# Hybrid decoder step: compression and block scores with their operands turned, one projection split in two roundings, constants in two loads

## The reference

```python
h = rms(x, norm1) * (1 + sc1) + sh1          # sc1, sh1 from c @ w_ada
z = h @ w_in                                  # 2856 columns: gq gk gv ga gr nq kc vc ks vs kw vw ng
log_a = log_sigmoid(ga @ w_gla_a + b_gla_a) / 16
o_g, state = gla(gq * 64 ** -0.5, gk, gv, log_a, state_gla)   # 4 heads, chunks of 16 tokens
o_g = rms(o_g, gla_norm) * silu(gr)
kc_c = rms(compress(kc, w_ck), kc_norm)       # blocks of 32 rows, step 16: 31 for the prompt
vc_c = compress(vc, w_cv)                     # einsum('bnjgd,jde->bnge', blocks, w)
o_n = g0 * cmp(qn, kc_c, vc_c) + g1 * selected(qn, ks, vs) + g2 * window(qn, kw, vw)   # g = sigmoid(ng)
x = x + g1_ * (concat(o_g, rms(o_n, nsa_norm)) @ w_out)
h2 = rms(x, norm2) * (1 + sc2) + sh2
x = x + g2_ * ((gelu(conv(h2 @ w_up)) * (h2 @ w_gate)) @ w_down)
```

## Time and profile before

| | us |
|---|---|
| three runs, lowest, median, highest | 997.56, 1007.92, 1012.57 |
| profiled execution, its own time | 995.57 |
| its span in the trace | 993.5 |
| PE busy in the span | 922.9 (93%) |
| DVE, ACT, POOL busy | 350.6, 356.7, 312.5 |
| mean granted PE clock | 0.955 |

### The profile page before, as it was taken

The page is one execution under the profiler, slowest core; times in us unless marked ns, Lnnn a source line. Parts: engine busy times, 40 slices in busy tenths (PEclk is TensorE's granted clock), DMA queues, the critical chain, the costliest instruction groups (busy, mean ns, idle before and its releaser), DMA issues.

```text
span 993.5 us, 16849 instructions
## 1 busy us (share of the span) xinstructions
PE 922.9 (93%) x6771; PEld 761.6 (77%) x6771; DVE 350.6 (35%) x816; ACT 356.7 (36%) x739; POOL 312.5 (31%) x235
## 2 busy tenths in 40 slices
PE   2899999999987999897879999999999999899998
PEld 0444667677875454665659989999999999899997
DVE  2207214423656788534242163222222222300001
ACT  4123134421332677547152354333333333212120
POOL 0003030402509100070633644334343331524240
PEclk9999989997875799999989999999999999999999
DMA  9922622304093700285826403222233332253430
GB/s 318 346 129 85 207 89 86 131 11 160 2 290 60 234 1 1 79 260 161 223 81 213 127 23 105 86 85 86 85 87 90 95 91 81 60 135 82 128 82 23
DMA packets 129293, 117.27 MB, mean 118 GB/s; under 512 B 13869, under 2 KB 107754, under 8 KB 128986
## 3 DMA queue, kind: packets, MB, share of 16 engines
q1 hardware_dynamic: 124496, 100.64, 33.8%
q0 software_dynamic: 4720, 15.55, 4.8%
HBM read 110.88 MB, written 9.45 MB: 121 GB/s over the span
## 4 chain that ended last, share of the span: by engine, by line
PE 82%; DMA 5%; DVE 5%; ACT 3%; POOL 2%; SPq 2%; issue 1%; DVEq 0%; ACTq 0%; POOLq 0%
PE bank L1507 14%; PE bank L1508 14%; PE bank L1509 14%; PE bank L902 6%; PE bank L1000 6%; PE bank L991 3%; PE bank L1214 3%; PE bank L977 3%; PE bank L984 3%; DMA z<-in_w_ada_dram 2%; PE bank L1314 2%; PE bank L1284 2%; PE bank L1116 1%; PE bank L943 1%; DMA cs<-constants 1%
## 5 line engine op out<-in xcount | busy, mean ns | idle before, releaser
L1508 PE MATMUL bank<-feat_r,ring_r 128*128 128x272 f32 x672 | 193.7, 288 | 0.0
L1507 PE MATMUL bank<-qk_r,ring_r 128*128 128x272 f32 x672 | 193.5, 288 | 0.0
L1509 PE MATMUL bank<-qk_r,ring_r 128*128 128x272 f32 x672 | 193.2, 288 | 0.0
L871 POOL TENSOR_TENSOR ring_r<-ring,ring_r 128x1024 fp32r<-128x1024 f32 x44 | 108.9, 2478 | 146.9 <-ACT ring_r L1943 146.9
L1509 PEld LDWEIGHTS bank<-qk_r,ring_r 128*128 128x128 f32 x672 | 126.5, 188 | 0.0
L1507 PEld LDWEIGHTS bank<-qk_r,ring_r 128*128 128x128 f32 x672 | 126.3, 188 | 0.0
L1508 PEld LDWEIGHTS bank<-feat_r,ring_r 128*128 128x128 f32 x672 | 126.0, 187 | 0.0
L1943 ACT ACTIVATE ring_r<-ring 128x1024 fp32r<-128x1024 f32 x44 | 46.1, 1053 | 88.5 <-DMA ring<-in_w_gate_dram 85.6
L848 POOL DMA_DIRECT2D z<-in_cache_kv_dram x64 | 34.2, 536 | 132.9 <-PE bank L902 93.5
L2557 DVE SCALAR_TENSOR_TENSOR z<-bank,conv,z 128x511 f32<-128x511 f32 x22 | 16.5, 750 | 134.3 <-ACT z L1970 134.3
L902 PE MATMUL bank<-cs,room 128*128 128x128 f32 (+3 forms) x293 | 42.2, 285 | 20.5 <-DMA room<-in_nsa_norm_dram 11.8
...
## 6 DMA issues: line engine op xcount, KB each, us to landing
...
```

The costliest lines, as they stand in the source:

```text
L871: pool.tensor_tensor(rounded(low), low, high_part(high), ALU.subtract).then_inc(u_split, 1)
L1507: pe.matmul(dst, rounded(high), rounded(x_high), start=first, stop=False)
L1508: pe.matmul(dst, rounded(high), rounded(x_low), start=False, stop=False)
L1509: return pe.matmul(dst, rounded(low), rounded(x_high), start=False, stop=last)
```

## The change

Five things change.

- `SPLIT` gets the gqk piece as its first entry. The four gqk units become three products of 8 rounded matmuls, as gv has. ACT rounds the gqk weights before it reads out the first unit, POOL makes their rest, and DVE makes the rest of the features right after unit 3 instead of after unit 8. `sample_rows(0)` and `sample_columns(0)` move from units 8 and 9 to units 0 and 1.
- The gate bias becomes a 17th row of `wga`, with a row of ones as 17th row of `gaT`; L1087 goes.
- The late constants are loaded in two parts. The part behind the states (`STATES` to `CW`, with `pair` in it) is loaded ahead of the ada piece 7; the other part (`dist`, `cbias`, `cmask`, half of `sbias`) stays where the whole was.
- Compression is turned: 32 block columns of `kT` are stationary and 128 columns of `wp` move, the offset j choosing one of four bands. Bands and halves are summed by `fold`; the values need 16 such matmuls. Block scores are turned too: `kcn` is stationary, the queries move in 512 columns into four bands, and the result is copied out and turned back by 8 transposes. `vrep` goes.
- DVE's order around it changes: `praw` and `kcn` come ahead of the norm of the keys, the gates go behind the block scores, and the scaling of the GLA output goes to POOL, behind its last small DMA.

```diff
-                        ("seqmask", NB), ("dist", SEQ), ("cbias", QT * G * R * 32), ("cmask", QT * 32), ("pair", P),
-                        ("sbias", PAST), ("nbias", TURNS * NS), ("wbias", WIN), ("dcbias", NCS + 1),
+                        ("seqmask", NB), ("dist", SEQ), ("cbias", QT * G * R * 32), ("cmask", QT * 32),
+                        ("sbias", PAST), ("pair", P),
...
+STATES = EC + NB * 2 * DV
...
-        gaT = at(5504, TOK, rows=16)
+        gaT = at(5504, TOK, rows=17)
...
-        ROW_NTH = [4, 2, 3, 5, 6, 7]
-        BAND_NTH = 1
-        UH, US, FH = 4 * KD // 2, 4, KD
-        SPLIT = ROWED[2:]
+        ROW_NTH = [1, 3, 4, 5, 6, 7]
+        BAND_NTH = 2
+        UH, US, FH = 5 * KD // 2, 5, KD
+        SPLIT = [ROWED[0]] + ROWED[2:]
...
                 if item == ("a", 7):
                     sp.wait_ge(unit_out, 23)
+                    sp.wait_ge(ld_consts, 16)
+                    sp.dma_start(cs[:, STATES:CW], cst[:, STATES:CW]).then_inc(ld_consts, 16)
                 if item == ("a", 9):
                     sp.wait_ge(*KC2_DONE)
                     load_block_weights()
                 if item == ("a", 10):
                     sp.wait_ge(st_gla, 32)
-                    sp.dma_start(cs[:, EC:CW], cst[:, EC:CW]).then_inc(ld_consts, 16)
+                    sp.wait_ge(ld_consts, 32)
+                    sp.dma_start(cs[:, EC:STATES], cst[:, EC:STATES]).then_inc(ld_consts, 16)
...
+                if n == 6:
+                    ones_row = cst[0:1, CC["tri"][0]:CC["tri"][1]]
+                    sp.dma_start(gaT[16:17, 0:SEQ].rearrange("p (t n) -> p t n", n=P), among(ones_row, QT)).then_inc(ld_small, 16)
+                    sp.dma_start(gaT[16:17, SEQ:TOK], ones_row[:, 0:NS]).then_inc(ld_small, 16)
...
+            pool.wait_ge(mx_act, TILES + 2)
+            for t in range(TILES):
+                m = ROWS[t]
+                og = z[0:m, t, 0:512].rearrange("p (h d) -> p h d", d=DV)
+                pool.tensor_tensor(og, og, spread(gss[0:m, t, 0:H], DV), ALU.mult).then_inc(hb_ok, 1)
...
+                elif dst[0] == "gqk":
+                    i, cols_ = SPLIT.index(n), slice(c0, c0 + width)
+                    for k in range(KD):
+                        pe.wait_ge(fh_ok, k + 1)
+                        pe.wait_ge(u_high_ok, KD // 2 * i + k // 2 + 1)
+                        pe.matmul(b[:, :], rounded(w_in_high(n, k)[:, cols_]), rounded(qk[:, k, 0:SEQ]), start=(k == 0), stop=False)
+                    pe.wait_ge(u_split, i + 1)
+                    for k in range(KD):
+                        pe.matmul(b[:, :], rounded(w_in_raw(n, k)[:, cols_]), rounded(qk[:, k, 0:SEQ]), start=False, stop=False)
+                    for k in range(KD):
+                        pe.wait_ge(fl_ok, k + 1)
+                        last = pe.matmul(b[:, :], rounded(w_in_high(n, k)[:, cols_]), rounded(feat[:, k, 0:SEQ]),
+                                         start=False, stop=(k == KD - 1))
...
                 unit_product(u)
+                if u == 0:
+                    pe.wait_ge(feat_ok, 6)
+                    sample_rows(0)
+                if u == 1:
+                    sample_columns(0)
                 if u == 2:
+                    pe.wait_ge(samp_ok, 1)
...
-                pe.matmul(dst, gaT[:, t * P:t * P + ROWS[t]], wga[:, :], start=True, stop=False)
-                last = pe.matmul(dst, const("tri", 1)[:, 0:ROWS[t]], bga[:, :], start=False, stop=True)
+                last = pe.matmul(dst, gaT[:, t * P:t * P + ROWS[t]], wga[:, :], start=True, stop=True)
...
-                compress(lambda g: bank[b + g][:, 0:32], kv,
-                         lambda part, j: kT[part, kv, j:j + CST * 31 + 1:CST]).then_inc(cmp_pe, 1)
+                for j in range(CST):
+                    for g in range(G):
+                        part, band_ = slice(g * DH, (g + 1) * DH), slice(j % 4 * BAND, (j % 4 + 1) * BAND)
+                        ins = pe.matmul(bank[b + g][band_, 0:P], kT[part, kv, j:j + CST * 31 + 1:CST], wp[kv][part, j, :],
+                                        start=(j < 4), stop=(j >= CST - 4), skip_group_check=True)
+                ins.then_inc(cmp_pe, 1)
...
             compressed(1, 6)
-            pe.wait_ge(cmp_dve, 1)
-            fold(lambda part: bank[6][part, 0:NCP], lambda g, h: praw[:, 1, g, h:h + NCP]).then_inc(cmp_pe, 1)
             pe.wait_ge(ld_wk, 64)
             compressed(0, 4)
+            pe.wait_ge(cmp_dve, 2)
+            for h in range(2):
+                for g in range(G):
+                    last = pe.matmul(bank[4][g * DH:(g + 1) * DH, 0:NCP], praw[:, 0, g, h * DH:(h + 1) * DH],
+                                     const("fold")[:, h:h + NCP], start=(h == 0), stop=(h == 1), skip_group_check=True)
+            last.then_inc(cmp_pe, 1)
+            for g in range(G):
+                for h in range(2):
+                    for r in range(R):
+                        last = pe.matmul(bank[7][r * 32:r * 32 + 32 - h, g * DH:(g + 1) * DH],
+                                         const("fold")[:, h:32], praw[:, 1, g, h * DH:(h + 1) * DH],
+                                         start=(h == 0), stop=(h == 1), skip_group_check=True)
+            last.then_inc(cmp_pe, 1)
+            pe.wait_ge(ld_consts, 32)
+            pe.wait_ge(cmp_dve, 3)
+            pe.matmul(bank[6][:, 0:NCP], const("pair"), ksq[:, 0:NCP], start=True, stop=True).then_inc(cmp_pe, 1)
             pe.wait_ge(kv_ok, 1)
             pe.wait_ge(mod_ok, 9)
             selected_columns(Z_KS, 1)
-            pe.wait_ge(cmp_dve, 3)
-            fold(lambda part: bank[4][part, 0:NCP], lambda g, h: praw[:, 0, g, h:h + NCP]).then_inc(cmp_pe, 1)
-            flip(bank[7][:, 0:P], vrep.rearrange("p a b -> p (a b)")).then_inc(cmp_pe, 1)
             selected_columns(Z_KW, 2)
-            pe.wait_ge(ld_consts, 32)
-            pe.wait_ge(cmp_dve, 4)
-            pe.matmul(bank[6][:, 0:NCP], const("pair"), ksq[:, 0:NCP], start=True, stop=True).then_inc(cmp_pe, 1)
             pe.wait_ge(qT_ok, R + 1)
             for j, c in enumerate((Z_KS, Z_KW)):
                 last = flip(bank[0][:, j * NS:(j + 1) * NS], z[0:NS, QT, c:c + P], NS)
             last.then_inc(k_t, 1)
-            pe.wait_ge(cmp_dve, 6)
-            pe.wait_ge(kT_ok, 5)
-            for t in range(QT):
-                for r in range(R):
-                    for g in range(G):
-                        last = pe.matmul(bank[4 + g][:, t * P + r * 32:t * P + (r + 1) * 32],
-                                         qT[g * DH:(g + 1) * DH, r, t * P:(t + 1) * P],
-                                         kcn[g * DH:(g + 1) * DH, :], start=True, stop=True)
+            pe.wait_ge(cmp_dve, 4)
+            for r in range(R):
+                for g in range(G):
+                    part = slice(g * DH, (g + 1) * DH)
+                    last = pe.matmul(bank[4 + g][r * 32:(r + 1) * 32, :], kcn[part, :], qT[part, r, 0:SEQ],
+                                     start=True, stop=True, skip_group_check=True)
+            last.then_inc(cs_out, 1)
+            pe.wait_ge(cpt_ok, 2)
+            for g in range(G):
+                for t in range(QT):
+                    last = flip(bank[4 + g][:, t * P:(t + 1) * P], cpt[:, g, t * P:(t + 1) * P])
             last.then_inc(cs_out, 1)
 
...
+            weights_high(0)
             for n in range(0, EARLY, 2):
                 unit_out_of_bank(n)
+                if n == 0:
+                    sample_rows_out(0)
...
-            a.wait_ge(cmp_pe, 6)
+            a.wait_ge(cmp_pe, 5)
             root(krs[:, 0:NCP], bank[6][:, 0:NCP], 1.0 / DH).then_inc(cmp_act, 1)
+            a.wait_ge(cs_out, 1)
+            a.activation(cpt[:, 1, :], bank[5][:, :], ACT.Copy).then_inc(cpt_ok, 1)
...
+                    v.wait_ge(unit_out, 4)
+                    v.wait_ge(sr_out, BAND_NTH)
+                    for k in range(KD):
+                        v.wait_ge(fh_ok, k + 1)
+                        v.tensor_tensor(rounded(feat[:, k, 0:SEQ]), feat[:, k, 0:SEQ], high_part(qk[:, k, 0:SEQ]),
+                                        ALU.subtract).then_inc(fl_ok, 1)
+                    v.wait_ge(samp_out, 2)
...
-            v.wait_ge(cmp_pe, 1)
-            for g in range(G):
-                last = v.tensor_copy(praw[:, 1, g, :], bank[6 + g][:, 0:32])
-            last.then_inc(cmp_dve, 1)
+            mod_group(8)
+            for kv, b in ((1, 6), (0, 4)):
+                v.wait_ge(cmp_pe, 2 - kv)
+                for g in range(G):
+                    last = v.tensor_copy(praw[:, kv, g, :], bank[b + g][:, 0:P])
+                last.then_inc(cmp_dve, 1)
+            v.wait_ge(cmp_pe, 3)
+            link(v.tensor_copy(kcn[:, 0:NCP], bank[4][:, 0:NCP]))
+            v.tensor_tensor(ksq[:, 0:NCP], kcn[:, 0:NCP], kcn[:, 0:NCP], ALU.mult).then_inc(cmp_dve, 1)
             v.wait_ge(qrs_ok, 2)
...
-            v.wait_ge(mx_act, TILES + 2)
-            for t in range(TILES):
-                m = ROWS[t]
```

(7 more changed lines are left out.)

114 lines of the change are left out of this document (42 added, 72 removed).

## The result

The changed kernel took 991.37 us (median of 4 runs, 986.8 to 994.4) beside 1005.84 us before (4 runs, 997.56 to 1012.57): ratio 0.9886, 95% interval 0.9838 to 0.9935. Six more runs later gave 994.69 us and a ratio of 0.9865 (0.9795 to 0.9935). All ratios here leave out, of each kernel, the runs over 1.5% above its fastest, so they aren't the quotients of the medians beside them.

What follows compares the result with a forecast made beforehand. PE was taken to bound the kernel, with 82% of the last chain. Terms −4.8 − 2.2 − 1.8 + 0.3 = −8.5 us, applied to the median 1007.92, gave 999.4 us; range 989 to 1008, forecast chance 0.55.

Steps and rivals of the forecast that it cites:

- The gqk units: Early PE units: four units in rounded products at 5.68 us each, −5.2 us, with a 0.4 us wait −4.8 us.
- The wait for the gv load: After the gqk units: PE reaches the next piece before it lands, 0.9 us of slack becoming a 0.4 us wait.
- Rival 2: gqk units bring nothing, as DVE's late read-out behind the silu chain sets the first gv unit: 1004.2 us, chance 0.10.
- The gate bias: Gate products on PE: five bias products at 0.43 us each go, −2.2 us, with ends 0 and −4.4.
- five L1110 in about 2.5 us: Sign in the new profile: the five gate products on PE take about 2.5 us.
- The block stage: From the keys' product to DVE's bias add: −2.5 us, less 0.7 for the moved gates, sum −1.8 us.
- the price of the turned products: Block stage: key product and turned scores at 3.6 us each at half clock, priced from banded 128-row products.
- Rival 1: Clock comes back in the block stage as denser products keep full clock: 5 us more gain, 994.4 us, chance 0.18.
- Rival 3: Block stage bands don't overlap with 64 rows and strided weights: 20.4 us more, 1019.8 us, chance 0.07.
- The scaling on POOL: First attention turns: five POOL instructions, some 6.8 us, lengthen DVE's work beside them by 31%, +0.3 to +0.4 us.
- Rival 4: POOL holds up DVE wholly in attention: 2.1 us instead of 0.3, 1001.2 us, chance 0.10.
- Constants: Loads for block stage and attention: ending the `pair` wait worth nothing, possible ada piece delay taken as 0, end 5.5 us.

Runs made afterwards that it cites:

- experiment 1: Changed kernel with the gqk units taken back to plain products, the rest kept: ratio to before 0.9996, 6.3 ± 1.0 us above the changed kernel at equal clock.
- experiment 3: Changed kernel with the GLA output scaling back on DVE, in its idle time: ratios to before 0.9856 and 0.9887, 1.8 ± 1.0 us below changed at equal clock.
- experiment 5: Changed kernel with the two-input scaling still on POOL, but earlier, in its wait for constants: ratio to before 0.9898, 2.5 ± 0.8 us below changed at equal clock.

## Why the prediction held, and where it was right by luck

The forecast was −8.5 us and 999.4; measured at equal clock −8.8, by the medians −14.5 and 991.4, inside the range. The 999.4 stood on a median of three runs, 1007.92; 63 runs of before have 1005.5, which is 2.4 of the 8 us by which it was off, and the clock of the first four runs of the changed kernel (0.9495 against 0.9447, at 8.1 us for 0.01) another 3.9.

- **The gqk units**, −4.8: 4.95 us in the trace. The wait for the gv load came as forecast, and DVE's read-out was in time. Rival 2 is refuted, also by the 6.3 us of experiment 1.
- **The gate bias**, −2.2: 2.96 us in the trace, 3.5 ± 1.3 by the undone version. The low piece of the clock stayed, as forecast. But I priced all five bias products at the 0.43 us of the first, and two of them lay in the low piece, at 0.99, so the term was 0.8 us too small. The sign "five L1110 in about 2.5 us" was off too; they take 3.2.
- **The block stage**, −1.8: the step that failed is the price of the turned products. I took 3.6 us each at half clock, from products with 128 rows; they took 1.97 and 1.96 us at half clock. That is 1.6 us twice, and the part from the keys to the bias add is 5.9 us shorter (20.54 to 14.64), not 2.5. All the rest of that chain was right: the start on the weights' DMA, the norm of the keys next on the chain, two copies, the turns back. The gates behind the scores cost 0.3, not 0.7.
- **Rival 1**, the clock coming back: false but for the keys' product of the second profile, worth 0.8 us. The clock was 0.50 from 278 to 298 us; the forecast's half clock was right, and about as much as rival 1's 5 us came from the shorter products instead. **Rival 3**, bands that don't overlap, was to decide at 125 ns a record; the keys took 31.
- **The scaling on POOL**, +0.3: the other step that failed. Attention took 88.50 us instead of 83.77, +4.7 (3.7 in the second profile), of which 3 to 4 are the held instruction (experiment 3). I had priced it by one pair of tensor-tensor rows, 31% longer; a tensor-scalar of DVE on SBUF was held wholly, over three to four POOL instructions. Rival 4 named this mechanism with 2.1 us; it was in every profile of the changed kernel, and larger. The Trainium skill's GPSIMD Engine Reference, Key points, names two kinds of DVE instruction that contend with POOL, those with two SBUF inputs and those in a two-port mode; the page VectorE: DVE Perf Modes, section Mode 2×_2P, puts a tensor-scalar from SBUF to SBUF in that mode. In the trace before, L2341, the same instruction, takes 0.34 us for 128 columns and 0.54 for 512, 0.52 ns for each further column, where a tensor-tensor takes about 1.04 (0.68 us for 512, 1.21 for 1024). I had read only the first kind into the rows. The runs agree with both kinds (experiment 5 for two inputs), and show besides that POOL's own column form hardly holds DVE.
- **Constants**, 0: no product waits for a late ada piece (L957 at 231.41 has no bracket), and `pair` is awaited by nobody.

The wrong terms nearly cancel, 3.4 + 0.4 us too little gain in the block stage and 0.8 in the gate against 4.4 too little loss (3.4 by the second profile), and so the sum was right by luck. From the keys' start to the end of attention the change brings 0.9 us (112.93 to 112.06; 2.6 in the second profile) where moving the norm and the scaling brings 7 to 9 (106.17, 104.20).

What stays open: what sets the place and length of the low pieces of the clock, which move between runs of one kernel by more than any term here (behind attention alone, three of the 14 profiles take 591 us and the other eleven 596 to 600), and why PE's wait for POOL at L991 is 1.4 us in some profiles and 3.0 in others, with a slower unit behind the longer wait each time (3.4 to 3.8 us for records that take 2.1 behind the shorter).
